# Closing norm inside the experts' arms, rounding and adds ahead in their queues, and a new fixed order for the recurrence

## The reference, cut to what matters

```python
for l in range(DEPTH):                                  # DEPTH = 2
    mix = mixer_sublayer(h, ...)                        # three kinds of attention, then o @ w_out
    h = layer_norm(DEEPNORM_ALPHA * h + mix, ln1_g[l], ln1_b[l])
    ffn = grouped_moe(h, router_w, router_bias, exp_w_gate[l], exp_w_up[l], exp_w_down[l])
    h = layer_norm(DEEPNORM_ALPHA * h + ffn, ln2_g[l], ln2_b[l])

def grouped_moe(h, router_w, router_bias, w_gate, w_up, w_down):
    scores = jax.nn.sigmoid(h @ router_w)               # 16 experts in 4 groups
    # group with the largest sum of its best two (score + bias), in it the best two experts,
    # gates = their scores over their sum
    for e in range(N_EXPERTS):
        a = jax.nn.silu(h @ w_gate[e]) * (h @ w_up[e])
        y = y + dense_gates[:, e:e + 1] * (a @ w_down[e])

def ssd_chunked(x, dt, a, b_in, c_in):                  # 2 chunks of 128, 16 heads, 2 groups
    acs = jnp.cumsum(adt, axis=-1)                      # adt = dt * a
    seg = jnp.exp(jnp.where(causal, acs[..., :, None] - acs[..., None, :], -jnp.inf))
    cb = jnp.einsum('bclgn,bcsgn->bcgls', cr, br)
    y_diag = jnp.einsum('bcgjls,bcsgjp->bclgjp', cb[:, :, :, None] * seg, xr)
    states = jnp.einsum('bclgn,bclgjp->bcgjpn', br, xr * decay_to_end[..., None])
    # state carried over the chunks; y_off = cr . state_in * exp(acs)
    return y_diag + y_off
```

## Time and profile before

| | us |
|---|---|
| three timed runs | 2313.51, 2322.91, 2326.73 (median 2322.91) |
| the profiled execution | 2300.37 |
| its span | 2298.6 |
| PE busy | 2144.3 (93%) |
| DVE busy | 1517.4 (66%) |
| ACT busy | 1237.3 (54%) |
| POOL busy | 70.0 (3%) |
| mean granted clock of PE | 0.966 |

### The profile page before, as it was taken

How to read it: one execution, slowest core, us unless ns; L and a number is a source line. 1 busy time by engine, 2 the same in 40 slices (tenths; PEclk the granted TensorE clock), 3 DMA queues, 4 the chain that set the end, 5 groups by cost and what they waited for, 6 DMA issues and landing times.

```text
span 2298.6 us, 32280 instructions
## 1 busy us (share of the span) xinstructions
PE 2144.3 (93%) x12190; PEld 1859.6 (81%) x12190; DVE 1517.4 (66%) x2106; ACT 1237.3 (54%) x1954; POOL 70.0 (3%) x76
## 2 busy tenths in 40 slices
PE   6987999989987999989999998989999999899999
PEld 5776888867776777768899977789998998778998
DVE  6467999986567899985655757555555556655554
ACT  4453877864544777764444553544444445454443
POOL 0001000000001000000000002000000000000000
PEclk9998999998998999999999999989999999999999
DMA  6123999982224999975555452435554556133553
GB/s 236 62 75 110 347 362 354 363 322 88 92 92 148 345 349 352 347 276 165 175 191 184 149 169 88 147 101 191 184 185 160 189 184 203 56 129 117 187 186 116
DMA packets 124214, 446.86 MB, mean 194 GB/s; under 512 B 14320, under 2 KB 15472, under 8 KB 123120
## 3 DMA queue, kind: packets, MB, share of 16 engines
q1 hardware_dynamic: 124048, 444.68, 55.9%
HBM read 443.57 MB, written 1.05 MB: 193 GB/s over the span
## 4 chain that ended last, share of the span: by engine, by line
PE 48%; DVE 3%; ACT 2%; issue 1%; POOL 0%; DMA 0%; DVEq 0%; SPq 0%; ACTq 0%
PE bank L650 8%; PE bank L651 8%; PE bank L652 8%; PE bank L608 4%; PE bank L609 4%; PE bank L610 3%; PE bank L1048 3%; PE bank L1047 3%; PE bank L1049 3%; PE bank L2421 1%; PE bank L2403 1%; DVE lo L571 1%; PE bank L920 1%; DMA scr<-in_alibi 0%; ACT scr L1008 0%
## 5 line engine op out<-in xcount | busy, mean ns | idle before, releaser
L571 DVE TENSOR_TENSOR lo<-stage,hi 128x1024 fp32r<-128x1024 f32 (+1 forms) x834 | 976.9, 1207 | 277.4 <-ACT hi L559 250.3
L559 ACT ACTIVATE hi<-stage 128x1024 fp32r<-128x1024 f32 (+1 forms) x834 | 844.5, 1044 | 291.4 <-DMA stage<-in_exp 92.1
L650 PE MATMUL bank<-thi,hi 128*128 128x256 f32 x1504 | 428.0, 285 | 5.2 <-DVE tlo L726 3.2
L651 PE MATMUL bank<-tlo,hi 128*128 128x256 f32 x1504 | 427.0, 284 | 0.0
L652 PE MATMUL bank<-thi,lo 128*128 128x256 f32 x1504 | 427.0, 284 | 0.0
L650 PEld LDWEIGHTS bank<-thi,hi 128*128 128x128 f32 x1504 | 290.2, 193 | 8.6 <-issue 7.1
L651 PEld LDWEIGHTS bank<-tlo,hi 128*128 128x128 f32 x1504 | 290.1, 193 | 1.4
L652 PEld LDWEIGHTS bank<-thi,lo 128*128 128x128 f32 x1504 | 290.0, 193 | 0.0
L608 PE MATMUL bank<-hi,thi 128*128 128x512 f32 (+3 forms) x656 | 261.6, 399 | 17.7 <-DVE tlo L726 5.8
L609 PE MATMUL bank<-lo,thi 128*128 128x512 f32 (+3 forms) x656 | 255.2, 389 | 0.0
L610 PE MATMUL bank<-hi,tlo 128*128 128x512 f32 (+3 forms) x656 | 254.7, 388 | 0.0
(11 more groups left out here) (351 smaller groups left out, 2778.5 us busy)
## 6 DMA issues: line engine op xcount, KB each, us to landing
stage<-in_exp SPq DMA_DIRECT2D x384, 512.0 KB, 6.0
stage<-in_ffn SPq DMA_DIRECT2D x264, 512.0 KB, 5.0
stage<-in_wi_a SPq DMA_DIRECT2D x16, 512.0 KB, 6.5
stage<-in_wi_b SPq DMA_DIRECT2D x16, 512.0 KB, 5.1
stage<-in_mem_wkv SPq DMA_DIRECT2D x16, 512.0 KB, 5.9
stage<-in_xwq SPq DMA_DIRECT2D x16, 512.0 KB, 4.7
stage<-in_xwo SPq DMA_DIRECT2D x16, 512.0 KB, 5.0
stage<-in_ssd_xbc SPq DMA_DIRECT2D x12, 512.0 KB, 5.0
```

What stands on the lines that cost most here:

```text
L559: a.activation(self.hi[i % NR][:, x:y], self.stage[(2 * i + p) % (2 * NS)][:, :y - x], ACT.Copy).then_inc(*c.tick(("hi", i, p), sem="hi"))
L571: v.tensor_tensor(self.lo[i % NR][:, x:y], self.stage[(2 * i + p) % (2 * NS)][:, :y - x], self.hi[i % NR][:, x:y].bitcast(F32), ALU.subtra ...
L650: t.matmul(out, hi[:, ws], self.thi[:, xs], start=(k == 0), stop=False)
L651: t.matmul(out, hi[:, ws], self.tlo[:, xs], start=False, stop=False)
```

## The change

There are four parts.

- **The closing norm inside both arms.** `ln_var` and `ln_scaled` of the closing norm stand in each arm of DVE, `ln_pow` in each arm of POOL, and wait for their own inputs rather than for `joined(S)`.
- **The mixer's output added ahead of the next weights.** In the second turn DVE splits the next chunk after `ln_scaled` rather than before the adds.
- **x rounded ahead of the scores.** ACT rounds both halves of x before the sigmoid; DVE's two subtractions stand straight behind `ln_x`, ahead of the routing.
- **The recurrence's new order.** Fixed plans (`ordered`) replace `interleave` and `woven`. The decay's subtract, mask and exponential (DVE, POOL, ACT) become, on ACT alone, four `Relu` of 128 columns out of PSUM with scale −1 and the row's sum as bias, and one `Exp` of 512 columns with scale −1. The causal mask moves to `cb`, once, on DVE. "seg" of the first two blocks stands ahead of the state's product. In the second chunk the blocks go 2, 3, 0, 1. Two quarters of the `out_pool` product stand behind the second chunk's sums where one stood.

```diff
+def ordered(plan, steps):
+
+    for x in plan:
+        next(steps[x])
+    for x in steps.values():
+        run(x)
...
         for turn, n0, w, full in self.pieces(c, wo_a, 512, D):
-            self.split_dve(v, c)
+            if turn == 0:
+                self.split_dve(v, c)
             for tt in range(2):
...
                 if turn:
                     self.ln_var(v, c, S, tt)
         self.ln_scaled(v, c, S, y)
+        self.split_dve(v, c)
...
             a.activation(R["xhi"][tt], self.x(tt), ACT.Copy).then_inc(*c.tick((S, "xhi", tt)))
-            if tt == 0:
-                for w in c.need((S, "logits")):
-                    a.wait_ge(*w)
-                a.activation(R["sc"], self.bank[0][:, 0:32], ACT.Sigmoid).then_inc(*c.tick((S, "sc")))
+        for w in c.need((S, "logits")):
+            a.wait_ge(*w)
+        a.activation(R["sc"], self.bank[0][:, 0:32], ACT.Sigmoid).then_inc(*c.tick((S, "sc")))
...
+        for tt in range(2):
+            for w in c.need((S, "xhi", tt)):
+                v.wait_ge(*w)
+            v.tensor_tensor(R["xlo"][tt], self.x(tt), R["xhi"][tt].bitcast(F32), ALU.subtract).then_inc(*c.tick((S, "xlo", tt)))
...
-        def rest(tt):
-            for w in c.need((S, "xhi", tt)):
-                v.wait_ge(*w)
-            v.tensor_tensor(R["xlo"][tt], self.x(tt), R["xhi"][tt].bitcast(F32), ALU.subtract).then_inc(*c.tick((S, "xlo", tt)))
-        rest(0)
...
-        rest(1)
         arms(v, c, self.flag[0:1, 0:1], (S, "flag"), lambda: self.compact_dve(v, c, l), lambda: self.dense_dve(v, c, l), S)
-        for w in c.need(joined(S)):
-            v.wait_ge(*w)
-        self.ln_scaled(v, c, S, R["y"])
+        for tt in range(2):
+            c.K.at[S, "scaled", tt] = c.last
...
-        arms(g, c, self.flag[0:1, 0:1], (S, "flag"), lambda: self.mem_norm(g, c, (S, "compact"), l, 5), lambda: self.dense_pool(g, c, l), S)
+        def compact():
+            self.mem_norm(g, c, (S, "compact"), l, 5)
+            self.ln_pow(g, c, (S, "compact"))
+        arms(g, c, self.flag[0:1, 0:1], (S, "flag"), compact, lambda: self.dense_pool(g, c, l), S)
         for w in c.need(joined(S)):
             g.wait_ge(*w)
-        self.ln_pow(g, c, S, joined=True)
...
@@ -2042,7 +2049,8 @@
...
-            self.ln_var(v, c, S, tt)
+            self.ln_var(v, c, V, tt)
+        self.ln_scaled(v, c, V, R["y"])
...
+        self.ln_pow(g, c, (S, "dense"))
...
+            seg(0, 0, (S, "Bt"))
+            seg(0, 1, (S, "cb"))
+            yield
             for g in range(2):
-                for w in c.need((S, "xd"), (S, "cb"), (S, "dte") if g == 0 else (S, "xs", 3)):
+                for w in c.need((S, "xd"), (S, "Bt"), (S, "dte") if g == 0 else (S, "xs", 3)):
                     t.wait_ge(*w)
...
-            for tt in range(2):
-                def quarter(tt, hb):
-                    yield
-                    for w in c.need((S, "ab", tt, hb), ((S, "ysum", 0, hb) if hb < 2 else (S, "seg", 0, hb)) if tt else
-                                    [(S, "Bt"), (S, "cb"), (S, "sts", 0), (S, "sts", 1)][hb]):
...
-                for i, _ in enumerate(woven([quarter(tt, hb) for hb in range(4)], 4)):
-                    if i % 2:
-                        yield
-                for g in range(2):
...
-        interleave([pool(), core()], 2)
-        run(last)
...
+            for hb in (2, 3, 0, 1):
+                seg(1, hb, (S, "ysum", 0, hb) if hb < 2 else (S, "seg", 0, hb))
...
+            for g in range(2):
+                ysum(1, g)
...
+        ordered("ppcpcpcpppcpcccppcpcpcpp", {"p": pool(), "c": core()})
...
+            def decay(tt, hb):
+
+                for w in c.need((S, "seg", "mm", tt, hb), (S, "acs"), (S, "ysum", "mm", 0, hb // 2) if tt else (S, "band", 3)):
+                    a.wait_ge(*w)
+                for j in range(4):
+                    h = hb * 4 + j
+                    a.activation(M[:, h * 128:(h + 1) * 128], self.bank[4 + hb][:, j * 128:(j + 1) * 128], ACT.Relu,
+                                 bias=R["acs"][:, tt * 16 + h:tt * 16 + h + 1], scale=-1.0).then_inc(*c.tick((S, "seg", tt, hb)))
+                for w in c.need(c.last):
+                    a.wait_ge(*w)
+                m4 = M[:, hb * 512:(hb + 1) * 512]
+                a.activation(m4, m4, ACT.Exp, scale=-1.0).then_inc(*c.tick((S, "mexp", tt, hb)))
+            decay(0, 0)
+            decay(0, 1)
+            yield
             for g in range(2):
                 for w in c.need((S, "st", "mm", g)):
...
-            for tt in range(2):
...
-                    m4 = M[:, hb * 512:(hb + 1) * 512]
-                    for w in c.need((S, "mseg", tt, hb)):
-                        a.wait_ge(*w)
-                    a.activation(m4, m4, ACT.Exp).then_inc(*c.tick((S, "mexp", tt, hb)))
-                    yield
-                for i, _ in enumerate(woven([quarter(tt, hb) for hb in range(4)], 4)):
-                    if i % 2:
-                        yield
-                    if tt and i == 0:
...
-        interleave([pool(), core()], 2)
-        squares(1)
-        run(last)
+            decay(0, 2)
+            decay(0, 3)
+            yield
+            for hb in (2, 3, 0, 1):
...
+            squares(0)
+            yield
+            squares(1)
+            yield
+        ordered("ppcpcpcpppcpcccpppcpcpp", {"p": pool(), "c": core()})
...
+            v.tensor_tensor(r3(R["cb"], 128), r3(self.bank[5][:, :], 128), bc(self.tri, 1, 4), ALU.mult).then_inc(
+                *c.tick((S, "cb")))
+            yield
...
-            for tt in range(2):
-                def quarter(tt, hb):
-                    h4 = slice(tt * 16 + hb * 4, tt * 16 + hb * 4 + 4)
-                    m3 = r3(M[:, hb * 512:(hb + 1) * 512], 128)
-                    for w in c.need((S, "seg", "mm", 0, hb) if tt else None):
-                        v.wait_ge(*w)
-                    v.tensor_copy(r3(self.gb_[:, hb * 512:(hb + 1) * 512], 128), bc(adt[:, h4], 2, 128)).then_inc(
...
-                    for w in c.need((S, "seg", "mm", tt, hb), (S, "ysum", "mm", 0, hb // 2) if tt else (S, "band", 3)):
-                        v.wait_ge(*w)
-                    v.tensor_tensor(m3, r3(self.bank[4 + hb][:, :], 128), bc(acs[:, h4], 2, 128), ALU.subtract).then_inc(
-                        *c.tick((S, "seg", tt, hb)))
...
-                    g = hb // 2
-                    for w in c.need((S, "mexp", tt, hb), (S, "cb")):
-                        v.wait_ge(*w)
-                    v.tensor_tensor(m3, m3, bc(R["cb"][:, (2 * tt + g) * 128:(2 * tt + g + 1) * 128], 1, 4), ALU.mult).then_inc(
-                        *c.tick((S, "M", tt, hb)))
-                for i, _ in enumerate(woven([quarter(tt, hb) for hb in range(4)], 4)):
-                    if i % 2:
-                        yield
-                    if tt and i == 1:
-                        self.rms_dve(v, c, S, ("y", 0), 2, 512, 1e-6, 176)
-                    if tt and i == 6:
-                        scaled(0)
...
+            def decayed(tt, hb):
+                m3, g = r3(M[:, hb * 512:(hb + 1) * 512], 128), hb // 2
+                for w in c.need((S, "mexp", tt, hb), (S, "cb")):
+                    v.wait_ge(*w)
+                v.tensor_tensor(m3, m3, bc(R["cb"][:, (2 * tt + g) * 128:(2 * tt + g + 1) * 128], 1, 4), ALU.mult).then_inc(
+                    *c.tick((S, "M", tt, hb)))
...
-                    yield
-        interleave([pool(), core()], 2)
-        self.split_dve(v, c)
-        self.rms_dve(v, c, S, ("y", 1), 2, 512, 1e-6, 184)
-        scaled(1)
+            for w in c.need((S, "dln")):
...
+            ab(0, 0)
+            ab(0, 1)
+            yield
+            for w in c.need((S, "cums")):
+                v.wait_ge(*w)
+            v.tensor_copy(acs, self.bank[6][:, 0:32]).then_inc(*c.tick((S, "acs")))
...
+            steps(0)
...
+            ab(0, 2)
+            ab(0, 3)
+            yield
+            decayed(0, 0)
+            decayed(0, 1)
+            yield
+            decayed(0, 2)
+            decayed(0, 3)
+            for hb in (2, 3, 0, 1):
+                ab(1, hb)
+            steps(1)
+            yield
+            summed(0)
+            yield
+            for hb in (2, 3, 0, 1):
+                decayed(1, hb)
+            self.rms_dve(v, c, S, ("y", 0), 2, 512, 1e-6, 176)
+            scaled(0)
+            yield
+            summed(1)
+            self.rms_dve(v, c, S, ("y", 1), 2, 512, 1e-6, 184)
+            scaled(1)
+            yield
+        ordered("ppppcppcpcpccppcpcpcpp", {"p": pool(), "c": core()})
```

169 lines of the change are left out of this document (65 added, 104 removed).

## The result

| | us |
|---|---|
| changed kernel, first four runs | 2290.19 to 2296.71, median 2293.48 |
| kernel before beside them | 2313.51 to 2326.73, median 2319.67 |
| ratio, 95% interval | 0.9886, 0.9852 to 0.9921 |
| the same with more runs side by side (7 and 18) | 2290.93 and 2311.88, ratio 0.9918, 0.9889 to 0.9947 |
| the profiled executions | 2293.15, before 2300.37 |

A forecast was written before the change was run, and what follows sets the result against it. PE, 93% busy, was taken to bound the kernel, so gains come only from its waits or lower clock. Terms −2.8 + 0.2 + 0.2 − 10.9 = −13.3 took the median 2322.91 to 2309.6 us; range 2298 to 2322.

The forecast's parts named there:

- the base: Whole kernel: savings summed against the profiled 2300.37 us, then carried to the timed runs' median 2322.91, 1.0% above.
- Closing norm, layer 0: End of layer 0's experts: PE's transposes start at 515.2 rather than 518.01, −2.8 us; bounds −3.8 to 0.
- The 0.5 us of slack for DVE's jump: Layer 0's exit: after its jump, DVE is ready for L1574 at 519.4, with 0.5 us to spare.
- Layer 1: End of layer 1's experts: L726 waits for DVE's jump, 1030.85 against 1030.71, +0.2 us.
- Mixer's output first: Experts' front: transposes 1.2 us earlier, but the split collides with POOL's work, so scores start 1.4 us later.
- +0.1 per layer: Experts' fronts: sum of moved split +1.4 and rounding −1.2, +0.2 us in all; bounds −0.8 to +1.5 per layer.
- x rounded ahead: Experts' front: the second low part (1.23 us) leaves the way between selection matrix and gather, −1.2 us per layer.
- Recurrence: Recurrence: −8.4 us of PE's 14.16 us of waits and −2.5 of clock, −10.9 us; bounds −15 and −3.
- I count −2.5: Recurrence clock: half of four 0.50 stretches vanish, each costing up to 1.65 us; counted as −2.5 us.
- the one of the tables: Recurrence rival: alternating `Relu` and `Exp` tables cost 20.5 us, giving 2330; chance 0.09 shared with a worse front.
- The rival of ACT as the bound: Recurrence rival: ACT at 0.49 us per 128 columns, recurrence −6.5, whole −9, giving 2314; chance 0.18.
- The balance "without slack": Recurrence, second chunk: ACT's chain, 10.0 us with split and DVE, just balances PE's other work.

The follow-up runs named there:

- the one with idle products: Changed kernel plus 58 idle 128x128 products per layer in PE's four waits at the experts' front: mean span 2289.6 ± 2.1 us against 2293.7 ± 2.2.
- the turned rows first: Changed kernel with the split moved to the group-count gap, plus DVE taking the turned rows before pool's last step: mean span 2283.9 ± 1.9 us in its four runs.
- the doubled `Relu`: Changed kernel with each second-chunk block's four `Relu` made twice, 16 more ACT instructions: recurrence stage 71.0 us, PE waits 4.30 us at the sums.
- the order alone: Changed kernel's recurrence order, but decay again by DVE's subtraction, POOL's mask and ACT's exponential: recurrence stage 73.1 us, against 79.9 to 82.1 in the kernel before.
- the chain alone: Old recurrence order, but decay made by ACT alone with `Relu` and `Exp`: recurrence stage 84.4 us, against 79.9 to 82.1 in the kernel before.

## Why the prediction was wrong

The place and the sign were right for three of the four parts; the base and the clock's terms failed. The forecast missed the first four runs' 2293.5 by 16.1 us: 11.6 are the base, and some 4 the size of the change, 17.3 rather than 13.3.

- **The base.** The step "carried to the median of the timed runs, 2322.91" failed. That median of three lay 11.6 us above the mean of 66 further runs, and the profiled execution 11 below it. From a base of 2311.3 (2309.5 and 1.8 around the span) the same −13.3 gives 2298.0, and the range moved with it (2286 to 2310) holds 2293.5. I had taken the 1% between profile and timed runs for an offset; it was the spread of one and the same program, which goes in good part with its clock.
- **Closing norm, layer 0:** −2.8 forecast, −2.6 measured at the transposes (2.15 us in all eleven traces with the edit), −3.4 with the mixer behind. The 0.5 us of slack for DVE's jump was there. **Layer 1:** +0.2 against 0.0 (L733, before L726, 5.48 us after the variance both times, and 5.3 to 5.6 in every trace); as forecast, PE's later start was not the path. By the runs' means the exits are worth 7.4, and the 4 us beyond the traces are **not explained**.
- **Mixer's output first:** the norm came 1.2 earlier, as forecast. The split lasted 4.51 us, from 196.04 to 200.55, as forecast (193.0 to 197.5), and the scores started about 1.1 later after the last product (forecast 1.4). Together with the −1.2 of the rounding the sum's two terms came out at −0.1 per layer. What failed is "+0.1 per layer" as the whole: the fronts took 0.7 and 1.7 more on the mean of the traces, 2.2 each between the two profiled ones, and 4.5 together by the runs. I had put in the wait at its own length, and no term for the clock. PE waits 4.35 us in one piece there, the clock is at 0.50 from before that into the gather, and between the profiled traces the scores take 1.25 longer and the gather's first products 1.0. Part of that is chance in the trace of before: unchanged scores took 6.98 in 4 of 10 fronts. Undoing the split brings the shorter fronts back, in its one trace, and the clock with them (mean 0.9636). Behind the sum I had written that the Trainium skill's lock ("SBUF — State Buffer", "SBUF: two separate sides") could make each piece wait for a whole POOL instruction. The trace agrees with it, though only the second piece waited: the first ran from 196.04 to 197.26, as long as alone, and POOL's first instruction, issued beside it, lasted 3.21 rather than 2.35, to 199.47; the second piece lasted until 200.55, some 1.1 us behind that end, 3.38 in all; and POOL's next lasted 3.20. So the two took turns, and both lose.
- **x rounded ahead:** −1.2 forecast, −1.2 measured. The two subtractions fit into DVE's wait, and the gather no longer waits for them but for the selection matrix. From the first routing instruction to the gather it is 9.05 us in both fronts of all five traces without this edit and 7.87 in all twelve with it (the one with idle products left out). It doesn't show in the fronts' lengths, where the clock's differences are as large.
- **Recurrence:** −10.9 forecast, −12 to −14 measured in its own stage, −13 to −15 with the stage behind it. The waits left were 7.2, forecast 5.8: the closing turn's is 5.06, not 3.3, because I let DVE's splits lie beside PE's quarters, while two pairs (4.63) and two adds stand between the scaling and the turned rows:

```profile
1420.77 1.23 DVE L3171 TENSOR_TENSOR scr<-scr,st 128x1024 f32<-128x1024 f32 x1 [0.81 <-POOL st L812]
1421.91 4.63 DVE L578 TENSOR_TENSOR lo<-stage,hi 128x1024 fp32r<-128x1024 f32 x4
1426.45 1.48 DVE L1123 TENSOR_TENSOR X<-X,bank 128x512 f32<-128x512 f32 x2
```

  The mis-sized term is the clock: "I count −2.5", while PE's busy time fell by 4.9 us over the stage, and by 6.2 over the 335 products that end ahead of the fourth stretch. Of the four low stretches three went, where I had taken half away, and the one behind the closing turn became twice as long. With the turned rows first it went too, and the stage lost another 6 us in the trace. The rival of ACT as the bound fell with `Relu` at 0.28 us, and the one of the tables with a single load.
- The balance "without slack" was right (0.3 us in the trace, 0.4 by the doubled `Relu`). That the order alone brings half or more of the gain and the chain alone none was not foreseen: I had priced the chain as if it gained by itself.

## What to carry to other kernels

Before a sum of a few microseconds is put on a base, ask how far its own runs spread and whether the profiled one is typical; compare stages of the traces by equal products, and only what repeats. A wait on the tensor engine is worth more than its length, in both directions: price the clock behind it too. When two terms cancel in a stage's length, cut the stage at single instructions: the rounding's 1.2 us can't be read from the fronts' lengths, yet they stand in every trace. Work that is moved behind a norm needs a slot in which its engine is not wanted and no other engine slows it: here the same split made both fronts longer in one slot, and in another they were 3 us shorter than there.
